# First input projection as three rounded products with split operands, and modulation products with the weights stationary

## The chip, the cores and the metric

The kernel runs on one core of a Trainium2 chip. The metric is the device time of one launch in microseconds (us). A core has TensorE (PE, matrix products; its weight loads are listed apart as PEld), VectorE (DVE), ScalarE (ACT), GpSimd (POOL) and SyncE (SP, here only a DMA queue). Each runs its own instruction list in order and waits on semaphores for the others.

## The reference, cut to what matters

Two transformer blocks follow each other on 256 latent and 256 context tokens, width 1024, all in float32. The change touches the head of the first one:

```
sh_a, sc_a, gt_a, sh_m, sc_m, gt_m = split(silu(cond) @ ada_w + ada_b, 6)   # twice: c, c_ctx; 2 layers
h = rms_norm(x) * (1 + sc_a) + sh_a                                          # 512 rows x 1024
qa, ka, va, qb, kb, vb, ob, g = split(h @ w_in)     # 7 blocks of 512 columns, and 16 gate columns
```

qa, ka, va go to a windowed attention (8 heads of 64) and a context attention; qb, kb, vb, ob and the 16 gates g (4 kinds by 4 heads) to a bidirectional chunked recurrence (mLSTM), whose gates pass tanh, softplus and running sums. Both outputs are merged and projected by ab_w_out, and an MLP follows.

## The kernel before, in words

Weights come through a ring of three buffers ("slabs", 2 MB: 1024 rows by 512 columns). SP issues them in the order of one list, and a slab waits until the one three places earlier is used. The list begins with four slabs of ada_w (modulation part 0), then the eight of ab_w_in (seven of 512 columns, the last of 16), then eight (part 1) and twelve (part 2) of ada_w, then ab_w_out.

*Modulation* (`ada_matmuls`, L665). Both condition vectors are held stationary: `csil` holds silu(c), silu(c_ctx) in two of its 46 columns and zeros elsewhere, so that a slice of it puts slab i's result on rows 2i and 2i+1. One slab is eight products with 8 to 24 stationary columns and 512 moving columns (L680). In the trace each float32 product is two records. The bias enters by one more product (L674). ACT copies the rows out (L698), PE turns them (L709), DVE copies the columns (L719). The generator yields after each product, and `fill(pe, queue, n)` (L688) takes n of them and so puts them between other work: part 0 (32 products) in the prologue, part 1 two by two between the 32 attention units, part 2 as 24 products ahead of the gate decays and then two by two in the recurrence (`ml_pe`, L1177), 36 times.

*First projection* (`ab_in_pe`, L756; `rows_pe`, L557). Per slab and token tile (four of 128) eight float32 products accumulate in one PSUM bank, hT stationary, weights moving: 7 x 4 x 8 = 224 products. The 16 gate columns come last: four groups with 4 stationary columns, 8 products each (L763), in banks 4 to 7. ACT copies each bank out (L776 to L782), then the gates' tanh (L1035). DVE squares and reduces qa and ka beside that (L794, L796). After it eight normalised tiles are turned (L833) and scaled (L812), then attention begins: scores (L857), turned probabilities (L865), values (L877), filler.

*Split products elsewhere.* Later matrices already run as three products in the rounded type fp32r: ACT rounds a slab (high, L336), DVE subtracts (low, L343), and PE adds x_high·w_high, x_low·w_high and x_high·w_low (L380, L1366, L1381, L2249).

*After attention.* Softplus (ACT), decays (DVE, ACT), 48 small products (L1114, L1120), turns of qb and kb (L1165), then per head h of four: L1185, filler, L1191, DVE's masks (L1249), and eight steps L1202, L1203, L1205, filler. Then the merge (L1325) and ab_w_out (L557).

Of the kernel before, what the change touches and what calls it, by code (L numbers as in the profile page):

```python
# [106 lines left out]
def bidir_dual_stack(nc, a, out, scratch_mod, scratch_rpb, noted):  # L107
    const_at, n_const = constant_columns()

    with ExitStack() as ctx:  # L110
# [55 lines left out]
        sc = sb("sc", [P, 6, 512])  # L166
# [13 lines left out]
        with ExitStack() as same_place:  # L180

            hT = same_place.enter_context(nc.sbuf_tensor("hT", [P, KT, 2 * T], F32))
            ring = same_place.enter_context(nc.sbuf_tensor("ring", [P, RING, SLAB], F32))
            arena = same_place.enter_context(nc.sbuf_tensor("arena", [P, ARENA], F32))
        hT_parts = sb("hT_parts", [P, KT, 2 * T], F32R)
        ring_parts = sb("ring_parts", [P, RING, SLAB], F32R)
        arena_parts = sb("arena_parts", [P, ARENA], F32R)
        psum = ctx.enter_context(nc.psum_tensor("psum", [P, 8, 512], F32))
# [55 lines left out]
        plan_rows("ab_in", a["ab_w_in"][0], KT, 3600)  # L244
# [274 lines left out]
        def first_mod_dve(dve):  # L519
# [6 lines left out]
            for k in range(KT):  # L526
                dve.wait_ge(*when(("read", ("L0a", k // 2))))
                dve.wait_ge(*when(("read", ("C0a", k // 2))))
                for v in range(2):
                    h = hT[:, k, 256 * v:256 * v + 256]  # L530
                    shift = mcol(0, v, 0)
                    nc.vector.tensor_scalar(h, h, plus1[v][:, k:k + 1], shift[:, k:k + 1], ALU.mult, ALU.add)\
                        .then_inc(*up(dve, ("first", k) if v else None))

# [37 lines left out]
        csil = area(23136, KT, 46)  # L572
# [3 lines left out]
        def setup_sp(sp):  # L576
# [6 lines left out]
                .then_inc(landing("vec_b"), 16)  # L583

# [5 lines left out]
        def setup_pool(pool):  # L590
            nc.gpsimd.memset(csil, 0.0).then_inc(*up(pool, "csil zero"))
            pool.wait_ge(*latest(pool))
# [4 lines left out]
            for part, (layer, n0, ns, base) in enumerate(ADA_PARTS):  # L597
                for v in range(2):
                    nc.gpsimd.dma_start(adab[base + v:base + 2 * ns:2, :],
                                        a["ada_b"][layer, 512 * n0:512 * (n0 + ns)].rearrange("(i f) -> i f", f=512))\  # L600
                        .then_inc(landing(f"ada_b {part}"), 16)
# [14 lines left out]
            nc.gpsimd.dma_start(stat[0:4, 200:204], a["ab_gate_b"][0].rearrange("(a b) -> b a", b=4), allow_slow_non_contiguous=True)\  # L616
                .then_inc(landing("gate_b"), 16)
# [21 lines left out]
        def setup_pe(pe):  # L639
            pe.wait_ge(*when(("dma", "const")))  # L640
            for i, (rows, ev) in enumerate(((ROWS_A, "vec_a"), (ROWS_B, "vec_b"))):
# [3 lines left out]
                nc.tensor.transpose(psum[:, i, 0:n], sc[0:n, i, 0:P], ident[0:n, 0:n]).then_inc(*up(pe, ("vec", "turned", i)))  # L645

        def setup_dve(dve):
            for i, (col, rows) in enumerate(((colA, ROWS_A), (colB, ROWS_B))):
# [3 lines left out]
                dve.wait_ge(*latest(dve))  # L652

        def setup_act(act):
            act.wait_ge(*when(("read", ("vec", 1))))
            act.wait_ge(*when("csil zero"))
            for i, name in enumerate(("c", "c_ctx")):
                nc.scalar.activation(csil[:, :, 22 + i], colB[:, ROWS_B[name]:ROWS_B[name] + 8], ACT.Silu).then_inc(*up(act, "silu c"))
                act.wait_ge(*latest(act))


        ADA_PARTS = ((0, 0, 4, 64), (0, 4, 8, 32), (1, 0, 12, 0))
        ADA_BANK = (2, 6, 0)

        def ada_matmuls(pe, part):  # L665
            layer, n0, ns, base = ADA_PARTS[part]
            rows = psum[0:2 * ns, ADA_BANK[part], :]
            stage(pe, "ada")
            pe.wait_ge(*bank(ADA_BANK[part], ("ada", part)))
            pe.wait_ge(*when("silu c"))  # L670
            pe.wait_ge(*when(("dma", f"ada_b {part}")))
            pe.wait_ge(*when(("dma", "const")))
            at = slice(base, base + 2 * ns)
            nc.tensor.matmul(rows, ident[at, at], adab[at, :], start=True, stop=False)  # L674
            for i in range(ns):
                name = (f"ada{layer}", n0 + i, 0)
                for k in range(KT):
# [4 lines left out]
                    if k == KT - 1:  # L682
# [11 lines left out]
        def ada_rows_act(act, part):  # L694
            stage(act, "ada")
            layer, n0, ns, base = ADA_PARTS[part]
            act.wait_ge(*when(("ada", "full", part)))
            nc.scalar.copy(adab[base:base + 2 * ns, :], psum[0:2 * ns, ADA_BANK[part], :])\  # L698
                .then_inc(*up(act, ("read", ("ada", part))))
            also(("ada", "rows", part), ("read", ("ada", part)))  # L700

        def ada_turn_pe(pe, part, b):
            stage(pe, "ada")
            layer, n0, ns, base = ADA_PARTS[part]
            at = slice(base, base + 2 * ns)
            pe.wait_ge(*when(("ada", "rows", part)))
            pe.wait_ge(*bank(b, ("mod", part)))
            for j in range(4):
                ins = nc.tensor.transpose(psum[:, b, 2 * ns * j:2 * ns * j + 2 * ns], adab[at, P * j:P * j + P], ident[at, at])  # L709
            ins.then_inc(*up(pe, ("mod", "turned", part)))  # L710

        def ada_turn_dve(dve, part, b):
            stage(dve, "ada")
            layer, n0, ns, base = ADA_PARTS[part]
            dve.wait_ge(*when(("mod", "turned", part)))
            src = psum[:, b, 0:8 * ns].rearrange("p (j i v) -> p v i j", j=4, v=2)
            for v in range(2):
                at = 48 * v + 4 * n0
                ins = nc.vector.tensor_copy(modcol[:, layer, at:at + 4 * ns].rearrange("p (i j) -> p i j", j=4), src[:, v])  # L719
                ins.then_inc(*up(dve, ("read", ("mod", part)) if v else None))  # L720
            dve.wait_ge(*latest(dve))

        def ada_store_pool(pool, part):
            stage(pool, "ada")
            layer, n0, ns, base = ADA_PARTS[part]
            pool.wait_ge(*when(("ada", "rows", part)))
            for v in range(2):
                nc.gpsimd.dma_start(scratch_mod[layer][v, 512 * n0:512 * (n0 + ns)].rearrange("(i f) -> i f", f=512),
                                    adab[base + v:base + 2 * ns:2, :])\
# [23 lines left out]
        AB = ("qa", "ka", "va", "qb", "kb", "vb", "so")  # L753
        rowg = ("i_f", "f_f", "i_b", "f_b")

        def ab_in_pe(pe):  # L756
            rows_pe(pe, "ab_in", lambda k, t: hT[:, k, P * t:P * t + P], range(4), KT, 3584, [0, 1, 2, 3], each="first")
            stage(pe, "ab")
            s = slab(pe, ("ab_in", 7, 0))
            for g in range(4):  # L760
                pe.wait_ge(*bank(4 + g, ("gates", g)))
                for k in range(KT):
                    ins = nc.tensor.matmul(psum[0:4, 4 + g, :], s[:, k, 4 * g:4 * g + 4], hT[:, k, :],  # L763
                                           start=(k == 0), stop=(k == 7))
                ins.then_inc(*up(pe, ("gates", "full", g)))
            also(("used", slab_at[("ab_in", 7, 0)]), ("gates", "full", 3))

        def ab_in_act(act):
            stage(act, "ab_in")
            for n, name in enumerate(AB):  # L770
                for t in range(4):
                    act.wait_ge(*when(("ab_in", "full", n, t)))
                    src = psum[:, t, :]
                    event = ("read", ("ab_in", n, t))
                    if name == "so":
                        ins = nc.scalar.activation(so[:, t, :], src, ACT.Sigmoid)  # L776
                    elif name == "kb":
                        ins = nc.scalar.activation(kb[:, t, :], src, ACT.Copy, scale=128 ** -0.5)
                    elif name == "vb":
                        ins = nc.scalar.copy(vb[:, t, :, 0:128], src.rearrange("p (h d) -> p h d", h=4))  # L780
                    else:
                        ins = nc.scalar.copy({"qa": qa, "ka": ka, "va": va, "qb": qb}[name][:, t, :], src)  # L782
                    ins.then_inc(*up(act, event))


        def qk_norm_dve(dve):
            stage(dve, "qk")
            for i in range(8):
                y = (qa, ka)[i % 2][:, i // 2, :].rearrange("p (h d) -> p h d", h=8)
                sq = sc[:, i % 2, :].rearrange("p (h d) -> p h d", h=8)  # L790
                dve.wait_ge(*when(("read", ("ab_in", i % 2, i // 2))))
                if i < 2:
                    dve.wait_ge(*when(("C0a", "turned", 3)))
# [3 lines left out]
                dve.wait_ge(*latest(dve))  # L797
            for i in range(8):
# [229 lines left out]
        def gates_act(act):  # L1028
# [3 lines left out]
            act.wait_ge(*when(("dma", "rpb rows")))  # L1032
            for g in range(4):
                act.wait_ge(*when(("gates", "full", g)))
                nc.scalar.activation(capped[g], psum[0:4, 4 + g, :], ACT.Tanh, bias=stat[0:4, 204 + g:205 + g],  # L1035
                                            scale=1 / 15.0).then_inc(*up(act, ("read", ("gates", g))))
# [2114 lines left out]
```

## Time and profile before

| | |
|---|---|
| median of 3 runs | 3432.3 us (3430.59 to 3435.97) |
| profiled execution | 3440.02 us, span 3438.2 us |
| PE busy | 3122.3 us, 91% of the span |
| DVE, ACT, POOL busy | 49%, 28%, 8% |
| mean granted TensorE clock | 0.941 |

The span is the stretch between the first and last instruction. A row of the view by windows reads: stretch, its length, then busy us (and instructions) of PE, PEld, DVE, ACT and POOL, the granted PE clock (1.00 is 2.4 GHz, 0.50 is 1.2 GHz), the busy share of the DMA engines, GB/s. A row of the timeline reads: start, us from first start to last end, engine, line, operation, out<-in, shape, count, and in brackets the idle time ahead. The duration of a matmul record includes its latency, so the cost of one in a stream is the distance from start to start.

### The profile page before, as it was taken

How to read it: one execution, taken by the hardware profiler on the slowest of the kernel's cores; microseconds unless marked ns; L12 is line 12 of the kernel's file. 1: busy time of each engine (PE TensorE's matmuls, PEld its weight loads, DVE VectorE, ACT ScalarE, POOL GpSimd, SP SyncE). 2: the span in 40 equal slices, each digit the busy share in tenths (PEclk: the TensorE clock that was granted, in tenths of full speed). 3: DMA queues.
4: the chain of work that ended last, by engine and by line, in shares of the span. 5: the costliest groups of instructions: out<-in, count | busy, mean ns of one | idle time of the engine just before them, and what ended most of it. 6: DMA issues, size and time to landing. Idle time of an engine off the chain costs nothing. (4 is left out here: it accounts for less than half of the span.)

```text
span 3438.2 us, 54550 instructions
## 1 busy us (share of the span) xinstructions
PE 3122.3 (91%) x24312; PEld 2324.8 (68%) x24312; DVE 1697.6 (49%) x2689; ACT 963.3 (28%) x1489; POOL 282.4 (8%) x362
## 2 busy tenths in 40 slices
PE   7999988799996977989978989999899999998899
PEld 2443333398994536888866979874579898455697
DVE  1104356465556108777755555455445453465453
ACT  1012310133331115443312333322223332142332
POOL 1202011000000012232310000000000000200000
PEclk9998989899998988999979999999999999999999
DMA  8311344245453210000024545542245554323253
GB/s 252 102 55 62 135 147 172 73 147 196 172 196 95 92 25 2 3 3 3 4 81 141 193 150 172 187 165 89 98 144 168 165 183 169 128 74 123 74 192 128
DMA packets 249827, 409.23 MB, mean 119 GB/s; under 512 B 10055, under 2 KB 102616, under 8 KB 249464
## 3 DMA queue, kind: packets, MB, share of 16 engines
q1 hardware_dynamic: 244824, 390.39, 33.3%
q0 software_dynamic: 4768, 15.35, 1.8%
q8 instruction: 191, 3.13, 0.4%
q14 instruction: 44, 0.36, 0.0%
HBM read 400.67 MB, written 2.95 MB: 117 GB/s over the span
## 5 line engine op out<-in xcount | busy, mean ns | idle before, releaser
L343 DVE TENSOR_TENSOR ring_parts<-ring,arena_parts 128x2048 fp32r<-128x2048 f32 x250 | 553.0, 2254 | 276.9 <-ACT arena_parts L336 274.6
L336 ACT CAST arena_parts<-ring 128x2048 fp32r<-128x2048 f32 x250 | 457.3, 1879 | 601.3 <-PE psum L2249 229.5
L2249 PE MATMUL psum<-arena_parts 128*128 128x256 f32 x2816 | 514.8, 286 | 6.4 <-DVE arena_parts L452 6.2
L2249 PEld LDWEIGHTS psum<-arena_parts 128*128 128x128 f32 x2816 | 444.0, 194 | 9.2 <-DVE arena_parts L452 9.2
L557 PE MATMUL psum<-ring,hT 128*128 128x512 f32 (+1 forms) x960 | 414.2, 593 | 9.1 <-DVE hT L1308 2.6
L2249 PE MATMUL psum<-arena_parts,ring_parts 128*128 128x256 f32 x1408 | 400.8, 285 | 0.0
L557 PEld LDWEIGHTS psum<-ring,hT 128*128 128x128 f32 x960 | 184.0, 192 | 234.5 <-issue 223.1
L380 PE MATMUL psum<-arena_parts 128*128 128x512 f32 x928 | 291.9, 396 | 8.3 <-DVE arena_parts L2285 8.1
L2249 PEld LDWEIGHTS psum<-arena_parts,ring_parts 128*128 128x128 f32 x1408 | 272.9, 194 | 0.0
L1381 PE MATMUL psum<-arena_parts 128*128 128x512 f32 x768 | 240.5, 395 | 7.8 <-DVE arena_parts L1428 7.8
L380 PEld LDWEIGHTS psum<-arena_parts 128*128 128x128 f32 x928 | 176.8, 191 | 46.6 <-DVE arena_parts L2285 9.0
L680 PE MATMUL psum<-ring,arena 128*24 128x512 f32 (+2 forms) x384 | 188.4, 625 | 3.1 <-DMA ring<-in_ada_w 3.1
L1366 PE MATMUL psum<-arena_parts 128*128 128x256 f32 x1024 | 187.9, 286 | 3.6 <-DVE arena_parts L446 3.6
L380 PE MATMUL psum<-ring_parts,arena_parts 128*128 128x512 f32 x464 | 182.6, 394 | 0.0
L1381 PEld LDWEIGHTS psum<-arena_parts 128*128 128x128 f32 x768 | 145.7, 191 | 38.5 <-DVE arena_parts L1428 8.4
L1366 PEld LDWEIGHTS psum<-arena_parts 128*128 128x128 f32 x1024 | 162.3, 195 | 5.1 <-DVE arena_parts L446 4.7
L1381 PE MATMUL psum<-ring_parts,arena_parts 128*128 128x512 f32 x384 | 151.3, 394 | 0.0
L1366 PE MATMUL psum<-arena_parts,ring_parts 128*128 128x256 f32 x512 | 146.0, 285 | 0.0
L2280 DVE TENSOR_TENSOR sc<-sc,psum 128x512 f32<-128x512 f32 x44 | 30.3, 688 | 228.5 <-PE psum L2249 228.5
L2731 PE MATMUL psum<-ring,hT 128*128 128x512 f32 x256 | 126.9, 626 | 1.3 <-DMA ring<-in_xmem_wkv 1.3
L416 POOL TENSOR_SCALAR stat<-stat 128x2 f32<-128x2 f32 x17 | 3.6, 210 | 1479.0 <-issue 1167.2
L471 PE MATMUL psum<-const,sc 128*128 128x128 f32 x240 | 52.9, 395 | 68.9 <-DVE sc L428 68.9
(407 smaller groups left out, 5095.4 us busy)
## 6 DMA issues: line engine op xcount, KB each, us to landing
ring<-in_mlp_w SPq DMA_DIRECT2D x48, 2048.0 KB, 7.8
ring<-in_ada_w SPq DMA_DIRECT2D x24, 2048.0 KB, 8.0
ring<-in_ffn_pre_w_gu SPq DMA_DIRECT2D x44, 1024.0 KB, 6.9
ring<-in_ffn_post_w_gu SPq DMA_DIRECT2D x44, 1024.0 KB, 7.1
ring<-in_ffn_pre_w_down SPq DMA_DIRECT2D x8, 2048.0 KB, 7.9
ring<-in_xmem_wkv SPq DMA_DIRECT2D x8, 2048.0 KB, 8.1
ring<-in_ffn_post_w_down SPq DMA_DIRECT2D x8, 2048.0 KB, 7.8
ring<-in_ab_w_in SPq DMA_DIRECT2D x7, 2048.0 KB, 8.3
```

The lines of the kernel that those rows point to most:

```text
L336: nc.scalar.copy(high_view(name)[:, k, :], raw_view(name)[:, k, :]).then_inc(*up(act, ("high", name, h)))
L343: nc.vector.tensor_tensor(low_view(name)[:, k, :], raw_view(name)[:, k, :], high_view(name).bitcast(F32)[:, k, :], ALU.subtract)\
L380: ins = nc.tensor.matmul(psum[:, b, :], lhs[q][:, k0 + k, P * t:P * t + P], s[:, k, :], start=(k0 + k == 0 and i == 0), stop=(k0 + k == kt ...
L416: nc.gpsimd.tensor_scalar(s[:, 2:4], s[:, 0:2], 1.0 / D, EPS, ALU.mult, ALU.add).then_inc(*up(pool))
L471: ins = nc.tensor.transpose(psum[:, b + 4, at:at + 128], sc[:, 2 * t + k // 4, 128 * (k % 4):128 * (k % 4) + 128], ident)
L557: ins = nc.tensor.matmul(psum[:, where[t], 0:w], lhs(k0 + k, tile), s[:, k, 0:w], start=(k0 + k == 0), stop=(k0 + k == kt - 1))
L680: ins = nc.tensor.matmul(rows, csil[:, k, 22 - 2 * i:22 - 2 * i + 2 * ns], s[:, k, :], start=False, stop=(i == ns - 1 and k == KT - 1))
L1366: ins = nc.tensor.matmul(psum[:, b, 256 * j:256 * j + 256], s[:, k, at:at + P], src[q][:, k, :], start=(k == 0 and i == 0), stop=(k == 7 a ...
L1381: ins = nc.tensor.matmul(psum[:, b, :], hid_groups[g % 2][q][:, k, P * t:P * t + P], s[:, k, :], start=(g == 0 and k == 0 and i == 0), sto ...
L2249: ins = nc.tensor.matmul(psum[:, b, 256 * j:256 * j + 256], s[:, k, at:at + P], x_parts[q][:, k, :], start=(k == 0 and i == 0), stop=(k == ...
L2280: nc.vector.tensor_tensor(t, t, psum[:, 2 * (n % 2) + 1, :], ALU.mult)\
L2731: ins = nc.tensor.matmul(psum[:, 6 + i, :], hT[:, k, 256 + P * i:256 + P * i + P], s[:, k, :], start=(k == 0), stop=(k == KT - 1))
```

## The change: what it does

- *First projection*: order of the blocks 0, 1, 2, 3, 4, 5, 7 (gates), 6. Each weight slab is split in two halves (k 0 to 3, 4 to 7): ACT rounds a half into `ab_high` (two places, one for each half), DVE writes the rest into `ring_parts`. The rows are split as well: ACT rounds hT[k] into `ab_high_x`, DVE subtracts in place. Three fp32r products take the place of each float32 one, over halves, so that all four token tiles of a block end with its second half. Blocks alternate between banks 0 to 3 and 4 to 7.
- *Gates*: DVE zeroes a 128-column area and puts the four groups at columns 0, 32, 64, 96; 24 products with 128 stationary columns give all of them in bank 4; tanh reads partitions 32g. Block 6 reuses the place that held the gates' high part.
- *Modulation*: the slab is stationary, 32 products per slab (8 k by 4 columns groups of 128) with 128 stationary and 2 moving columns. DVE adds the bias from a turned copy. One `fill` unit is now eight products, and a slab has four units: the fills are 17 in the prologue, 1 between attention units, 12 ahead of the decays, 1 in the recurrence. The turns to rows (parts 1 and 2, only for the gate vectors' use) and their ACT copies, POOL stores and waits move: part 1 ahead of the decays, part 2 after the merge.
- *DVE*: squares of qa, ka go between the splits of blocks 3 and 4.

```diff
-                for k in range(KT):
-                    s = slab(pe, name)
-                    ins = nc.tensor.matmul(rows, csil[:, k, 22 - 2 * i:22 - 2 * i + 2 * ns], s[:, k, :],
-                                           start=False, stop=(i == ns - 1 and k == KT - 1))
+                for j in range(4):
+                    s = slab(pe, name)
+                    at = 8 * i + 2 * j
+                    for k in range(KT):
+                        ins = nc.tensor.matmul(psum[:, b, at:at + 2], s[:, k, P * j:P * j + P], sil[:, k, :],
+                                               start=(k == 0), stop=(k == KT - 1))
...
+        def ab_high_act(act, n, h):
+            act.wait_ge(*when(("ab padded") if n == 7 else ("slab", slab_at[("ab_in", n, 0)])))
...
+            if n == 6 and h == 1:
+                act.wait_ge(*when(("ab used", 5, 1)))
+            elif n:
+                act.wait_ge(*when(("ab used", AB_ORDER[AB_ORDER.index(n) - 1], h)))
+            nc.scalar.copy(ab_high_at(n, h), ab_raw(n, h)).then_inc(*up(act, ("ab high", n, h)))
...
         def ab_in_pe(pe):
+            for i, n in enumerate(AB_ORDER):
+                for h in range(1 if n == 7 else 2):
+                    pe.wait_ge(*when(("ab low", n, h)))
...
+                    for k in range(4 * h, 4 * h + 4):
+                        for t in range(4):
+                            for j, (w, y) in enumerate(((high, ab_high_x), (high, hT_parts), (low, ab_high_x))):
+                                ins = nc.tensor.matmul(psum[:, b, :], y[:, k, tile], w[:, k - 4 * h, :],
...
-            fill(pe, ada[0], 16)
             first_turn_pe(pe, "L0a")
             fill(pe, ada[0], 8)
             first_turn_pe(pe, "C0a")
-            fill(pe, ada[0], 8)
-            fill(pe, ada[0], 1)
-            ada_turn_pe(pe, 0, 3)
+            fill(pe, ada[0], 9)
             ab_in_pe(pe)
             qk_norm_pe(pe)
-            att_pe(pe, "na", na, [("read", ("qkT", i)) for i in range(8)], ada[1], 2)
-            att_pe(pe, "cx", cxa, (), ada[1], 2)
+            att_pe(pe, "na", na, [("read", ("qkT", i)) for i in range(8)], ada[1], 1)
+            att_pe(pe, "cx", cxa, (), ada[1], 1)
             fill(pe, ada[1], 1)
-            fill(pe, ada[2], 24)
+            fill(pe, ada[2], 12)
+            ada_turn_pe(pe, 1, 7)
             decay_pe(pe)
```

## Rows read from the trace of the kernel before

**Rows 1.** Windows: the stretches that the change reaches.
```profile
54.20:276.00 221.80, 221.74 (x513) 91.14 (x513) 21.47 (x34) 19.79 (x32) 29.23 (x21) 0.99 0.31 88
286.90:310.90 24.00, 22.10 (x45) 8.57 (x46) 10.55 (x23) 7.07 (x16) 15.29 (x34) 0.50 0.00 0
311.20:371.30 60.10, 60.10 (x246) 24.90 (x243) 24.70 (x57) 19.11 (x49) 0.00 (x0) 1.00 0.31 105
371.40:428.50 57.10, 55.82 (x193) 19.82 (x192) 17.53 (x64) 16.95 (x64) 0.00 (x0) 0.97 0.43 148
428.60:450.30 21.70, 21.70 (x51) 4.97 (x50) 15.42 (x45) 4.30 (x6) 1.13 (x2) 1.00 0.82 286
467.70:593.00 125.30, 114.13 (x384) 44.95 (x384) 77.08 (x272) 5.04 (x8) 14.94 (x25) 0.92 0.39 134
```

**Rows 2.** Waits of PE from 50 to 620 us: total, times, longest.
```profile
PE psum L1202 <- DVE sc L1249: 11.2, 4, 2.8
PE psum L1114 <- ACT arena L1103: 4.4, 1, 4.4
```

**Rows 3.** Timeline: first modulation product, end of part 0, first projection product.
```profile
17.75 15.45 PE L680 MATMUL psum<-ring,arena 128*8 128x512 f32 x32 [3.06 <-DMA ring<-in_ada_w]
...
50.96 0.57 ACT L698 COPY adab<-psum 8x512 f32<-8x512 f32 x1 [6.17 <-PE psum L680]
...
54.26 66.31 PE L557 MATMUL psum<-ring,hT 128*128 128x512 f32 x150 [2.26 <-DVE hT L532]
```

**Rows 4.** Groups by line, PE, 54 to 276 us.
```profile
L557 PE MATMUL psum<-ring,hT 128*128 128x512 f32 x448 | 194.2, 596 | 2.3 <-DVE hT L532 2.3
L763 PE MATMUL psum<-hT,ring 128*4 128x512 f32 x64 | 27.6, 592 | 0.0
```

**Rows 5.** Timeline of a later split projection, 512 moving columns.
```profile
2271.40 0.62 PE L380 MATMUL psum<-arena_parts 128*128 128x512 f32 x2
...
2272.08 0.62 PE L380 MATMUL psum<-arena_parts 128*128 128x512 f32 x2
```

**Rows 6.** Groups of the page: the two steps of a split, half a slab.
```profile
L343 DVE TENSOR_TENSOR ring_parts<-ring,arena_parts 128x2048 fp32r<-128x2048 f32 x250 | 553.0, 2254 | 276.9 <-ACT arena_parts L336 274.6
L336 ACT CAST arena_parts<-ring 128x2048 fp32r<-128x2048 f32 x250 | 457.3, 1879 | 601.3 <-PE psum L2249 229.5
```

**Rows 7.** Timeline: products with 4 moving columns, and what follows.
```profile
458.18 3.55 PE L1120 MATMUL psum<-arena,const 4*128 4x4 f32 x16
461.66 5.15 PE L1165 MATMUL psum<-const,arena 128*128 128x128 f32 x32
```

**Rows 8.** Timeline: products with 64 moving columns, and what follows.
```profile
2316.62 3.68 PE L2429 MATMUL psum<-arena 128*128 128x64 f32 x32
2320.13 3.65 PE L2731 MATMUL psum<-ring,hT 128*128 128x512 f32 x8
```

**Rows 9.** Windows around the small products and the turns.
```profile
455.00:461.20 6.20, 6.20 (x47) 6.20 (x46) 0.00 (x0) 0.00 (x0) 0.00 (x0) 0.50 0.42 158
461.70:464.60 2.90, 2.90 (x15) 2.90 (x15) 0.32 (x1) 1.26 (x3) 2.06 (x4) 0.50 0.00 0
464.80:466.00 1.20, 1.20 (x14) 1.20 (x13) 0.00 (x0) 1.20 (x3) 1.01 (x3) 1.00 0.00 0
```

**Rows 10.** Timeline: one early attention unit, from its scores to its filler.
```profile
294.97 2.07 PE L857 MATMUL psum<-arena 64*128 64x512 f32 x2
296.98 1.11 PE L865 MATMUL psum<-const,sc 128*128 128x128 f32 x4
298.02 1.97 PE L877 MATMUL psum<-sc,arena 128*64 128x128 f32 x8
299.92 1.88 PE L674 MATMUL psum<-adab,const 16*16 16x512 f32 x2
```

**Rows 11.** Timeline: one early step of the recurrence.
```profile
475.38 0.80 PE L1202 MATMUL psum<-arena,sc 128*128 128x129 f32 x2 [2.79 <-DVE sc L1249]
...
476.97 3.60 PE L680 MATMUL psum<-ring,arena 128*24 128x512 f32 x4
480.50 0.80 PE L1202 MATMUL psum<-arena,sc 128*128 128x129 f32 x2
```

More of the change, by code:

```diff
@@ L533, in first_mod_dve, with low_x, first_high_act @@
                         .then_inc(*up(dve, ("first", k) if v else None))
+            def low_x(k):
+                dve.wait_ge(*when(("first high", k)))
+                nc.vector.tensor_tensor(hT_parts[:, k, :], hT[:, k, :], ab_high_x.bitcast(F32)[:, k, :], ALU.subtract)\
+                    .then_inc(*up(dve, ("first", "low", k)))
+            modulated(0)
+            for k in range(1, KT):
+                modulated(k)
+                low_x(k - 1)
+            low_x(KT - 1)
+        def first_high_act(act):
+            stage(act, "norm")
+            for k in range(KT):
+                act.wait_ge(*when(("first", k)))
+                nc.scalar.copy(ab_high_x[:, k, :], hT[:, k, :]).then_inc(*up(act, ("first high", k)))
         def rows_pe(pe, name, lhs, tiles, kt, n_total, banks, needs=(), only=None, each=None):
@@ L692, in fill, with ada_cols_dve @@
             stage(pe, held)
[L694 to L700, printed above, removed]
+        def ada_cols_dve(dve, part):
+            stage(dve, "ada")
+            layer, n0, ns = ADA_PARTS[part]
+            dve.wait_ge(*when(("ada", "full", part)))
+            src = psum[:, ADA_BANK[part], 0:8 * ns].rearrange("p (c v) -> p v c", v=2)
+            for v in range(2):
+                at = 48 * v + 4 * n0
+                nc.vector.tensor_tensor(modcol[:, layer, at:at + 4 * ns], src[:, v],
+                                        colC[:, 48 * layer + 4 * n0:48 * layer + 4 * n0 + 4 * ns], ALU.add)\
+                    .then_inc(*up(dve, ("read", ("ada", part)) if v else None))
+            also(("mod", part), ("read", ("ada", part)))
+            dve.wait_ge(*latest(dve))
@@ L702, in ada_turn_pe @@
         def ada_turn_pe(pe, part, b):
             stage(pe, "ada")
-            layer, n0, ns, base = ADA_PARTS[part]
-            at = slice(base, base + 2 * ns)
-            pe.wait_ge(*when(("ada", "rows", part)))
+            layer, n0, ns = ADA_PARTS[part]
+            pe.wait_ge(*when(("mod", part)))
             pe.wait_ge(*bank(b, ("mod", part)))
-            for j in range(4):
-                ins = nc.tensor.transpose(psum[:, b, 2 * ns * j:2 * ns * j + 2 * ns], adab[at, P * j:P * j + P], ident[at, at])
+            for v in range(ADA_ROWS[part][1]):
+                at = 48 * v + 4 * n0
+                ins = nc.tensor.transpose(psum[0:4 * ns, b, P * v:P * v + P], modcol[:, layer, at:at + 4 * ns], ident)
@@ L710, in ada_turn_pe, with ada_rows_act @@
             ins.then_inc(*up(pe, ("mod", "turned", part)))
[L712 to L721, printed above, removed]
+        def ada_rows_act(act, part, b):
+            stage(act, "ada")
+            layer, n0, ns = ADA_PARTS[part]
+            at, nv = ADA_ROWS[part]
+            act.wait_ge(*when(("mod", "turned", part)))
+            nc.scalar.copy(adab[0:4 * ns, at:at + P * nv], psum[0:4 * ns, b, 0:P * nv])\
+                .then_inc(*up(act, ("read", ("mod", part))))
@@ L723, in ada_store_pool @@
         def ada_store_pool(pool, part):
             stage(pool, "ada")
[L725 to L729, printed above, removed]
+            layer, n0, ns = ADA_PARTS[part]
+            at, nv = ADA_ROWS[part]
+            pool.wait_ge(*when(("read", ("mod", part))))
@@ new lines, in ab_low_dve, with ab_pad_dve @@
+        def ab_low_dve(dve, n, h):
+            stage(dve, "ab_split")
+            dve.wait_ge(*when(("ab high", n, h)))
+            nc.vector.tensor_tensor(ab_low(n, h), ab_raw(n, h), ab_high_at(n, h).bitcast(F32), ALU.subtract)\
+                .then_inc(*up(dve, ("ab low", n, h)))
+        def ab_pad_dve(dve):
+            stage(dve, "ab_split")
+            dve.wait_ge(*when(("slab", slab_at[("ab_in", 7, 0)])))
+            v = raw_view(("ab_in", 7, 0))
+            nc.vector.memset(v[:, :, P:2 * P], 0.0).then_inc(*up(dve))
+            dve.wait_ge(*latest(dve))
+            for g in range(4):
+                nc.vector.tensor_copy(v[:, :, P + 32 * g:P + 32 * g + 4], v[:, :, 4 * g:4 * g + 4])\
+                    .then_inc(*up(dve, "ab padded"))
@@ L766, in ab_in_pe @@
-            also(("used", slab_at[("ab_in", 7, 0)]), ("gates", "full", 3))
-        def ab_in_act(act):
[L769 to L783, printed above, removed]
@@ new lines, in ab_out_act @@
+        def ab_out_act(act, i):
+            n = AB_ORDER[i]
+            stage(act, "ab_in")
+            name = AB[n]
+            for t in range(4):
+                act.wait_ge(*when(("ab_in", "full", n, 3 if name == "so" else t)))
+                src = psum[:, t + (4 * (i % 2) if n != 6 else 0), :]
+                event = ("read", ("ab_in", n, t))
+                if name == "so":
+                    ins = nc.scalar.activation(so[:, t, :], src, ACT.Sigmoid)
+                elif name == "kb":
+                    ins = nc.scalar.activation(kb[:, t, :], src, ACT.Copy, scale=128 ** -0.5)
+                elif name == "vb":
+                    ins = nc.scalar.copy(vb[:, t, :, 0:128], src.rearrange("p (h d) -> p h d", h=4))
+                else:
+                    ins = nc.scalar.copy({"qa": qa, "ka": ka, "va": va, "qb": qb}[name][:, t, :], src)
+                ins.then_inc(*up(act, event))
@@ new lines, in ab_in_act, with ab_in_dve @@
+        def ab_in_act(act):
+            for i, n in enumerate(AB_ORDER):
+                if i < 7:
+                    ab_high_act(act, AB_ORDER[i + 1], 0)
+                if n == 7:
+                    gates_act(act)
+                else:
+                    ab_out_act(act, i)
+                if i < 7 and AB_ORDER[i + 1] != 7:
+                    ab_high_act(act, AB_ORDER[i + 1], 1)
+        def ab_in_dve(dve):
+            for n in AB_ORDER[1:]:
+                if n == 7:
+                    ab_pad_dve(dve)
+                ab_low_dve(dve, n, 0)
+                if n != 7:
+                    ab_low_dve(dve, n, 1)
+                if n in (3, 4):
+                    qk_squares_dve(dve, range(4 * n - 12, 4 * n - 8))
@@ L797, in qk_norm_dve @@
                 dve.wait_ge(*latest(dve))
+        def qk_norm_dve(dve):
+            stage(dve, "qk")
             for i in range(8):
@@ L1032, in gates_act @@
             act.wait_ge(*when(("dma", "rpb rows")))
+            act.wait_ge(*when(("gates", "full")))
             for g in range(4):
-                act.wait_ge(*when(("gates", "full", g)))
-                nc.scalar.activation(capped[g], psum[0:4, 4 + g, :], ACT.Tanh, bias=stat[0:4, 204 + g:205 + g],
-                                            scale=1 / 15.0).then_inc(*up(act, ("read", ("gates", g))))
+                rows = slice(32 * g, 32 * g + 4)
+                nc.scalar.activation(capped[g], psum[rows, 4, :], ACT.Tanh, bias=stat[rows, 204:205],
+                                            scale=1 / 15.0).then_inc(*up(act, ("read", "gates") if g == 3 else None))
                 act.wait_ge(*latest(act))
@@ L1135, in rope_pool @@
                 pool.wait_ge(*when(("ab_in", "full", 6, t)))
-            pool.wait_ge(*when(("gates", "full", 3)))
             for y in (qb, kb):
@@ L2922, in _ @@
             first_out_act(act)
-            ada_rows_act(act, 0)
+            for h in range(2):
+                ab_high_act(act, 0, h)
+            first_high_act(act)
             ab_in_act(act)
-            gates_act(act)
-            att_act(act, "na", na, 0.125, [("gates", "full", 3)])
+            att_act(act, "na", na, 0.125, [("ab_in", "full", 6, 3)])
             att_act(act, "cx", cxa, 0.125)
-            ada_rows_act(act, 1)
             softplus_act(act)
+            ada_rows_act(act, 1, 7)
             decay_act(act)
@@ L2989, in _ @@
             first_out_dve(dve)
-            ada_turn_dve(dve, 0, 3)
+            for h in range(2):
+                ab_low_dve(dve, 0, h)
+            ada_cols_dve(dve, 0)
             first_mod_dve(dve)
             gates_dve(dve)
+            ab_in_dve(dve)
             qk_norm_dve(dve)
```

129 lines of the change are left out of this document (83 added, 46 removed).

## The prediction

> **What bounds the kernel now.** I read the shares, then PE's waits, then windows over the stretches that the diff touches, then the timeline inside them, and last the granted clock. PE issues nearly without pause: 221.74 of 221.80 us in the first projection, all of the attention from 311 us on, 21.70 of 21.70 us in the filler ahead of the decays [rows 1]. Its waits between 50 and 620 us are few: 2.8 us per head of the recurrence and 4.4 us for the decays [rows 2]. So up to the merge the time is the sum of what PE issues, and everything is priced there. The reader is to see three more things. The projection's 448 and the gates' 64 records cost 0.43 us each (194.2/448, 27.6/64) [rows 4]. The clock is not the same everywhere: it is 0.50 (1.2 GHz) through the first 24 us of attention although PE is busy for 22 of them, and 1.00 after [rows 1]. And products with 4 moving columns ran at 0.50 for 6.20 us without one gap, while the 128-column turns behind them had the clock at 1.00 within about 3 us [rows 9].
>
> **First projection: less work.** 224 float32 products become 672 rounded ones. Three of these take 2272.08 - 2271.40 = 0.68 us, 0.227 each [rows 5]: 152.4 us, against 194.2. The gates go from 27.6 to 24 x 0.227 = 5.4 us. The splits: half a slab costs ACT 1.88 and DVE 2.25 us [rows 6], while PE works 10.9 us on a half (48 products). ACT's high part of the next block's second half waits for the end of the present block and for four copies of its banks; that is some 7 us with DVE's part, under the 10.9 us of the next first half. It is hidden, DVE's squares too. One place has no cover: block 6's first half needs the place of the gates' high part, which is free only when the gates are done. Then ACT 1.88 + DVE 2.25 + handovers = 4.4 us of idle PE (zero is excluded, nothing of PE's lies there; twice that if ACT is late). The clock may fall in such a gap; I add 1.7, an estimate: the 3 us or so that the turns took to raise it [rows 9], half of it lost. New length 163.9 us against 221.8: -58. Bounds: -62 (no clock loss) and -29 (each slab's splits exposed once, 7 x 4.1 us). The tail (turns L833, start of attention) keeps its shape.
>
> **Modulation: the same PE time at the high clock, twice that at the low one.** One slab was 16 records at 0.43 = 6.9 us. It is now 32 products of 128 stationary and 2 moving columns, 64 records. No row has 128 x 128 stationary and 2 moving. The nearest two: 64 moving columns at the high clock, (2320.13 - 2316.62)/32 = 0.110 us per record [rows 8]; 4 moving columns at the low clock, (461.66 - 458.18)/16 = 0.2175 [rows 7]. They differ by two, as the clocks do, and hardly by the moving columns, so the weight load sets them. A slab costs 7.0 us at 2.4 GHz and 13.9 us at 1.2 GHz. There is nothing to win at either, only the bias products go.
>
> The stationary block of the L1120 row has 4 rows, the new one 128. By the Trainium skill (TensorE: Matmul & The Clock Gate, section "LDWEIGHTS (loading the stationary operand)") a load takes time by its columns and not by its rows; by that the 0.2175 holds for the new products, and the L2429 row with its 128 rows, at half of it, agrees.
>
> So the question is the clock. What speaks: with 4 moving columns PE had no gap for 6.20 us and stayed at 0.50 [rows 9]. With 64-row scores, turns and 16-column filler it stayed at 0.50 for 24 us [rows 1]. I take it that the new products leave the clock low, as the small ones did; between the attention's own work (under 5 us per unit at the low clock [rows 10]) they then stand like pauses, and that stage needed 24 us to get to the high clock even with its old filler. I take 0.50 for the prologue, both attentions, the filler and the recurrence.
>
> - Prologue: first product at 17.75, end of part 0 at 50.9 [rows 3]. Now 4 slabs at 13.9 less some 4 us that the turns beside them hold the clock up, and 3.4 for the second turns: end at 73; the chain to the first projection product (bias add, plus one, modulate, round, subtract) is about 4.5 us where it was 3.3: 77.5 against 54.3. +23. Bounds -2 and +30.
> - First attention (84.4 us, of which 60.1 at 1.00 [rows 1]). A unit's own work at the low clock is 299.92 - 294.97 = 4.95 us [rows 10], plus 16 x 0.2175 = 3.48: 16 units are 135, +51. Where turns and values come together the clock may come back for a while: I take +43. Bounds -1 and +51.
> - Context attention (57.1). Less 32 x 1.72 of filler halves: (57.1 - 27.5)/16 = 1.85 own work, up to 3.4 at the low clock, plus 3.48: 110, +53. Gaps don't double: +43. Bounds -1 and +53.
> - Filler ahead of the decays: 21.7 + 4.4 = 26.1 us [rows 1, 2] was set by DVE's and ACT's decays. Twelve units are 41.8 us and now outlast them. ACT's copy of part 1's rows waits for PE's turn behind the filler, and the exponentials stand behind that copy, so the 4.4 comes again: 46.2, +20. With the high clock (20.9) nothing changes.
> - Recurrence: 125.3/4 = 31.3 us per head [rows 1]. A step at the low clock is 476.97 - 475.38 = 1.59 [rows 11] + 3.48 = 5.07; eight of them 40.6, one filler 3.5, L1185 1.7, four records of L1191 3.4, the wait 2.8 [rows 2]: 52. +20.8 per head, +83. Bounds -8 (DVE, busy 77.08 of 125.30 us [rows 1], sets a floor soon under the present pace) and +90.
> - After the merge DVE's columns of part 2, PE's turn and no ACT wait ahead of ab_w_out: +1. SP's list keeps its order and every slab its place; at 14 us a slab DMA has time.
>
> **Sum.** +23 - 58 + 43 + 43 + 20 + 83 + 1 = +155 us. On the profiled execution 3440.0 + 155 = 3595; it lies 7.7 above the median of the runs, so against the median 3432.3 + 155 = 3587. Faster in the projection, much slower in everything that the filler shares.
>
> **Rivals.**
> - *Loads hold the clock (faster).* The new filler keeps the granted clock as the old one did. For it: PE issues without a gap, and the 4-column rows have 4 stationary rows too, so they don't tell loads of 128 rows apart. Against: the 24 us at 0.50 with a busy PE. Prologue -1, projection -58, attentions -2, decays 0, recurrence -1, tail +1: -61, 3371. Decided at the first 12-unit filler: above 0.9 there, and it holds everywhere. Chance 0.28. The Trainium skill (same page, section "What's actually happening") says that the clock follows how busy PE has been recently and that activity releases the throttle; read plainly that is this rival, and rows 9 are what stands against it.
> - *Low clock only in the long runs.* The products of the attentions hold the clock between fillers; it falls in the prologue, the long filler and the recurrence: +23 - 58 - 2 + 20 + 83 + 1 = +67, 3499. For it: from 311 to 371 us the same products stood at 1.00. Chance 0.04. If the recurrence holds as well it is -16, 3416. Chance 0.02.
> - *The rounded products don't do what they say,* bound by the splits: the -29 above with the clock held, 3400. For it: two engines and a semaphore chain per half slab. Against: later stages do the same at 0.227. Chance 0.02.
>
> **How the numbers follow.** Forecast 0.64 at 3587, its own range 3535 to 3630 (the terms of attention and recurrence each between full cold and a third won back). Loads hold the clock 0.28, the others as above. Faster (by over 0.2%, which is about what a measurement tells from no change) holds in 0.28 + 0.02 + 0.02 = 0.32, slower in 0.64 + 0.04 = 0.68; I keep 0.01 of these for no change. To leave out no more than 2 in 10 the range has to hold the fast case: 3362 to 3630.
>
> **What would show it.** The windows of the new kernel: granted clock 0.5 in the 12-unit filler, which is then 42 us long; about 0.22 us per L1120-like record; the first projection's products 0.227 apart and one gap of some 4 us behind the gates; the first of them at 77 us; the recurrence's steps 5 us apart. Wrong would be: 0.11 us per modulation record and clock 1.0 in that filler (then 3371), or a projection that waits for low parts in each slab.

## The result, and the profile after

The changed kernel takes 3579.8 us (median of 4 runs, 3578.75 to 3581.53) against 3431.45 us (median of 4, 3427.79 to 3435.97). The ratio is 1.0432, 95% interval 1.0414 to 1.0450: slower by 148 us, in a forecast of +155. Its profiled execution took 3581.53 us, span 3579.7, mean granted TensorE clock 0.878 where it was 0.941.

First the shares and the slices of the span. Per engine: busy us, share of the span, instructions; then 40 equal slices, the granted clock in tenths.

```profile
PE 3264.0 (91%) x25634; PEld 2699.4 (75%) x25634; DVE 1733.9 (48%) x2721; ACT 995.9 (28%) x1511; POOL 281.3 (8%) x357
...
PEclk6985555579999899899997999999989999999899
```

PE is busy for 91% as before, but for 142 us more, and five slices in a row show half the clock. The windows say what stood there (stretch, length, busy us of PE, PEld, DVE, ACT, POOL, granted clock, DMA share, GB/s): first projection, first attention, context attention, filler, recurrence. They stand beside [rows 1].

```profile
78.70:249.80 171.10, 166.64 (x696) 134.26 (x697) 51.60 (x60) 45.16 (x49) 30.07 (x21) 0.97 0.40 114
262.10:387.60 125.50, 124.12 (x480) 93.42 (x478) 35.26 (x80) 25.03 (x64) 13.88 (x31) 0.54 0.15 51
387.60:485.30 97.70, 97.18 (x369) 76.49 (x369) 17.52 (x64) 17.37 (x63) 0.00 (x0) 0.50 0.25 87
485.40:529.80 44.40, 44.40 (x210) 44.40 (x210) 15.71 (x47) 3.85 (x5) 0.00 (x0) 0.50 0.41 142
557.00:742.40 185.40, 177.72 (x788) 169.72 (x788) 75.41 (x264) 3.78 (x6) 15.31 (x24) 0.50 0.26 91
```

The projection is 51 us shorter and runs at the high clock. Everything that shares PE with modulation products is longer, at 0.50 to 0.54, with PE busy nearly throughout. In the filler PE was busy for 44.40 of 44.40 us, loading for all of it, and had 0.50. The timeline (start, us from first start to last end) shows the pieces: both halves of the prologue, the first projection product, one unit of the context attention, the filler and what follows, one step of the recurrence.

```profile
17.95 26.54 PE L701 MATMUL psum<-arena,ring 128*128 128x2 f32 x128 [2.22 <-DMA ring<-in_ada_w]
44.35 3.65 PE L502 MATMUL psum<-const,arena 128*128 128x128 f32 x16
47.80 27.30 PE L701 MATMUL psum<-arena,ring 128*128 128x2 f32 x128
78.79 0.77 PE L850 MATMUL psum<-sc_parts,arena_parts 128*128 128x512 f32 x1 [3.69 <-issue]
...
442.58 1.22 PE L972 MATMUL psum<-arena 64*128 64x256 f32 x2
443.72 0.69 PE L980 MATMUL psum<-const,sc 128*128 128x128 f32 x2
444.34 1.12 PE L992 MATMUL psum<-sc,arena 128*64 128x128 f32 x4
445.39 3.58 PE L701 MATMUL psum<-arena,ring 128*128 128x2 f32 x16
...
485.36 44.53 PE L701 MATMUL psum<-arena,ring 128*128 128x2 f32 x208
529.75 0.59 PE L737 MATMUL psum<-const,modcol 128*32 128x128 f32 x2
535.39 3.58 PE L1232 MATMUL psum<-const,arena 4*128 4x4 f32 x32 [5.05 <-ACT arena L1221]
...
550.50 1.84 PE L701 MATMUL psum<-arena,ring 128*128 128x2 f32 x16
...
561.77 0.78 PE L1319 MATMUL psum<-arena,sc 128*128 128x129 f32 x2
562.34 0.64 PE L1320 MATMUL psum<-arena,sc 128*128 128x129 f32 x2
562.77 0.64 PE L1322 MATMUL psum<-sc,arena 128*128 128x129 f32 x2
563.20 3.42 PE L701 MATMUL psum<-arena,ring 128*128 128x2 f32 x16
566.48 0.78 PE L1319 MATMUL psum<-arena,sc 128*128 128x129 f32 x2
```

The filler's 208 records take (529.75 - 485.36)/208 = 0.213 us each. One unit happened to fall into a stretch at the high clock (550.50): 16 records in 1.77 us, 0.111 each. So the new product has the two prices of [rows 7] and [rows 8], and which one it has goes with the clock. PE's waits from 50 to 780 us (total, times, longest) hold few things that are new:

```profile
PE psum L1319 <- DVE sc L1366: 10.4, 4, 2.8
PE psum L1442 <- DVE arena L1418: 10.4, 4, 9.4
PE psum L1232 <- ACT arena L1221: 5.0, 1, 5.0
PE psum L850 <- DVE ring_parts L812: 4.4, 1, 4.4
PE psum L850 <- issue: 3.7, 1, 3.7
```

### The profile page after: what moved, and what is told of

It is laid out like the page before. It is cut to its first block and busy times, and to the rows that moved or that the text cites. A ratio compares the mean times of both kernels' runs of the same rounds, so it can differ in the third digit from the quotient of the medians.

```text
span 3579.7 us, 57242 instructions
## 1 busy us (share of the span) xinstructions
PE 3264.0 (91%) x25634; PEld 2699.4 (75%) x25634; DVE 1733.9 (48%) x2721; ACT 995.9 (28%) x1511; POOL 281.3 (8%) x357
## 5 line engine op out<-in xcount | busy, mean ns | idle before, releaser
L701 PEld LDWEIGHTS psum<-arena,ring 128*128 128x128 f32 x1536 | 327.3, 326 | 12.7 <-issue 12.7
L701 PE MATMUL psum<-arena,ring 128*128 128x2 f32 x1536 | 325.7, 345 | 2.2 <-DMA ring<-in_ada_w 2.2
L577 PE MATMUL psum<-ring,hT 128*128 128x512 f32 (+1 forms) x512 | 220.3, 592 | 4.3 <-DVE hT L2300 1.6
L577 PEld LDWEIGHTS psum<-ring,hT 128*128 128x128 f32 x512 | 98.6, 194 | 121.9 <-issue 114.6
```

Source lines behind the costliest of these rows:

```text
L577: ins = nc.tensor.matmul(psum[:, where[t], 0:w], lhs(k0 + k, tile), s[:, k, 0:w], start=(k0 + k == 0), stop=(k0 + k == kt - 1))
L701: ins = nc.tensor.matmul(psum[:, b, at:at + 2], s[:, k, P * j:P * j + P], sil[:, k, :], start=(k == 0), stop=(k == KT - 1))
```

## The experiments

Two theories. *Clock:* modulation products with 2 moving columns leave the clock low, and their low clock also doubles the work that stands between them; the projection gains by itself. *Rivals:* a 128 x 128 float32 load is slow at any clock; or the splits cost something that the sum doesn't hold. Each run was timed in rounds beside the kernel before on the same chip.

### Each part alone

`e1_projection_alone` puts the old modulation back:

```diff
-                        ins = nc.tensor.matmul(psum[:, b, at:at + 2], s[:, k, P * j:P * j + P], sil[:, k, :],
+                    ins = nc.tensor.matmul(rows, csil[:, k, 22 - 2 * i:22 - 2 * i + 2 * ns], s[:, k, :],
...
-            ada_cols_dve(dve, 0)
+            ada_turn_dve(dve, 0, 3)
```

> New projection (split operands, padded gates, squares between the splits) with the modulation as it was before: csil stationary, 512 moving columns, the fills and turns of before. Theory (the slowdown is the clock that the modulation products with 2 moving columns leave low): the projection is shorter by 52 us (50.6 measured, 2.4 of cold start in it back, 1 for rounding and subtracting ahead of it), everything behind it as before: 3431 - 52 = 3379, 3370 to 3388. The first attention runs at the clock of before. Rival (the splits on ACT and DVE or the rounded products cost part of the slowdown, here or behind the projection): 3400 or more.

Measured: 3379.68 us, ratio 0.9844 (0.9829 to 0.9859). `e2_modulation_alone` is the other half, the kernel before with the new modulation:

```diff
-                    ins = nc.tensor.matmul(rows, csil[:, k, 22 - 2 * i:22 - 2 * i + 2 * ns], s[:, k, :],
+                        ins = nc.tensor.matmul(psum[:, b, at:at + 2], s[:, k, P * j:P * j + P], sil[:, k, :],
```

> New modulation (slab stationary, 2 moving columns) with the float32 projection of before. Theory: all of the loss and none of the gain, so 3431 + 148 + 52 = 3631, 3620 to 3645, with the granted clock 0.5 in both attentions, in the filler ahead of the decays and in the recurrence. Rival (projection and modulation disturb each other, the parts don't add up): more than 15 us away from 3631.

Measured: 3634.04 us, ratio 1.0572 (1.0545 to 1.0599). The parts add up: -54 and +201 give +147, the change measured +148. The splits cost nothing that shows. The slices of the clock, first with the projection alone, then with the modulation alone:

```profile
PEclk9989998999998979999979999999899999998999
```

```profile
PEclk8996555559999989799897999999989999999899
```

The five slices at half the clock go with the modulation.

### The same products with more moved columns

`e3_128_moving` leaves the change as it is and only widens the moving operand:

```diff
-                        ins = nc.tensor.matmul(psum[:, b, at:at + 2], s[:, k, P * j:P * j + P], sil[:, k, :],
+                        ins = nc.tensor.matmul(psum[:, b, at:at + MOVED], s[:, k, P * j:P * j + P], wide[:, 2 * k:2 * k + MOVED],
```

> The changed kernel, except that each modulation product moves 128 columns in place of 2 (silu(c), silu(c_ctx) and 126 columns of later pairs and zeros, whose results are written beside and overwritten or not read). Same weight loads, same number of instructions. Theory (few moved columns leave the clock low): the clock is held, a record costs 0.11 us, which the load sets anyway, so more work for PE makes the kernel faster: 3377, 3365 to 3390; granted clock above 0.9 in the 13-unit filler. Rival (a load of 128 x 128 float32 costs 0.21 us here at any clock, or stationary weights from the ring are slow for another reason): stays at 3580 or above.

Measured: 3377.84 us, ratio 0.9837 (0.9822 to 0.9852); once more, on another chip (`e3_again`), 3377.27, 0.9827 (0.9813 to 0.9840).

> The kernel with 128 moving columns once more, on the same chip as the other three, so that differences of a few us can be read: 3378.

Sixty-four times as many columns moved, none of the added ones of use, make the changed kernel 202 us faster. The filler, in the timeline and as a window:

```profile
375.14 23.49 PE L706 MATMUL psum<-arena,ring 128*128 128x128 f32 x208
```

```profile
375.20:398.60 23.40, 23.40 (x211) 23.35 (x210) 15.72 (x47) 3.86 (x5) 0.00 (x0) 1.00 0.77 268
```

The number of records is that of the change, 0.112 us apart at clock 1.00. The rival of slow loads falls: the loads are the same. With 32 columns:

> As the run with 128 moving columns, but 32. Theory: it is the amount of moved columns that counts, and a quarter of the engine's time moving them is still too little where nothing else stands beside them: clock 0.5 in the 13-unit filler, somewhat better in the attentions; 3540, 3480 to 3580. Rival (2 columns were a special case, any real number of columns holds the clock): about 3377, as with 128.

Measured: 3545.99 us, ratio 1.0358 (1.0301 to 1.0414). The filler stays where it was, (490.08 - 445.69)/208 = 0.213 us per record. What is won lies in the first attention, which took 348.74 - 259.66 = 89.1 us where the change took 126.7.

```profile
445.69 44.58 PE L706 MATMUL psum<-arena,ring 128*128 128x32 f32 x208
```

### 64 columns: a miss, and what it taught

> As the run with 128 moving columns (gates in the place that the change gave them), but 64. With 32 the clock stood at 0.5 in the 13-unit filler and the time was 3546. Theory (the amount of moved columns decides, and it is a step, not a slope: a stretch runs at one of two clocks): 64 is enough, 3377 as with 128, the record set by its load at 0.11 us. Rival (the time slopes with the columns): half way, about 3480.

Measured: 3522.64 us (3513.89 to 3538.11), ratio 1.0264 (1.0238 to 1.0290). Neither theory holds. In its trace one kind of record has two prices:

```profile
45.11 3.62 PE L502 MATMUL psum<-const,arena 128*128 128x128 f32 x16
48.52 14.48 PE L706 MATMUL psum<-arena,ring 128*128 128x64 f32 x128
...
429.47 3.68 PE L706 MATMUL psum<-arena,ring 128*128 128x64 f32 x16
434.13 44.64 PE L706 MATMUL psum<-arena,ring 128*128 128x64 f32 x208
```

Both groups run without a gap. The first, behind turns (L502) at whose end the clock had risen, goes at 0.113 us per record (14.48/128); the second came in at the low clock and stays there at 0.215 (44.64/208). What stood ahead seems to decide. But the number of columns counts at the same place too. Behind the same turns, first with 2 columns (`e2_modulation_alone`), then with 32 (`e4_32_moving`), the products began at the high clock as well and had lost it by 52 us, with PE busy throughout, where those with 64 kept it for all of 14.5 us:

```profile
48.30:51.00 2.70, 2.70 (x26) 2.70 (x26) 0.00 (x0) 0.59 (x1) 0.00 (x0) 1.00 1.05 405
52.00:55.00 3.00, 3.00 (x15) 3.00 (x16) 0.00 (x0) 0.00 (x0) 0.00 (x0) 0.50 0.04 12
```

```profile
48.80:51.00 2.20, 2.20 (x23) 2.20 (x21) 0.00 (x0) 0.81 (x2) 0.00 (x0) 1.00 1.05 410
52.00:55.00 3.00, 3.00 (x16) 3.00 (x16) 0.00 (x0) 1.24 (x1) 0.00 (x0) 0.50 0.33 116
```

`e9_64_after_128` tests what a raised clock is worth to 64 columns, by a few wide units at the places where it had been lost:

```diff
+        WARM = {1: (16, 17, 18), 2: (0, 1, 2, 13, 14, 22, 23, 31, 32, 40, 41)}
...
+                    MOVED = P if 4 * i + j in WARM.get(part, ()) else 64
```

> The expectation for 64 columns failed (3523 in place of 3377). Its trace has the same products at both clocks: 0.113 us apart behind turns that had raised the clock (second half of the prologue, most of the first attention), 0.215 apart for 44.6 us in the filler, which it entered with the clock low. New theory: 64 moved columns are enough to keep a raised clock but not to raise it. Here 11 to 14 of the 96 units move 128 columns (the first three of the context attention, the first three of part 2, the second and third step of the recurrence in each head), all others 64. Theory: these raise the clock and the 64 behind them keep it: context attention 58 us, filler 26, recurrence near 130; the prologue's first half stays cold, which is 13 us more than with 128 throughout: 3396, 3385 to 3415. Rival (64 columns lose the clock after a while whatever came before; what was held in the first attention was held by the attention's own products): above 3480.

Measured: 3392.83 us (3388.56 to 3405.34), ratio 0.9890 (0.9870 to 0.9910). Fourteen units of 96 differ from the run with 64 columns, and 130 us are gone. The context attention's first unit with 128 columns is slow, the second fast, and those with 64 behind it stay fast; so do the filler (its wide ones are its second to fourth, the clock was up when it began; a timeline row names only the first shape of its group) and the steps of the recurrence:

```profile
355.10 3.36 PE L707 MATMUL psum<-arena,ring 128*128 128x128 f32 x16
...
359.97 2.05 PE L707 MATMUL psum<-arena,ring 128*128 128x128 f32 x16
...
367.08 2.00 PE L707 MATMUL psum<-arena,ring 128*128 128x64 f32 x16
...
406.61 23.44 PE L707 MATMUL psum<-arena,ring 128*128 128x64 f32 x208
...
457.93 3.07 PE L707 MATMUL psum<-arena,ring 128*128 128x128 f32 x16
461.51 1.95 PE L707 MATMUL psum<-arena,ring 128*128 128x128 f32 x16
463.96 1.90 PE L707 MATMUL psum<-arena,ring 128*128 128x64 f32 x16
```

Behind the wide units the rival, a clock that 64 columns lose after a while, does not hold: the context attention kept it from its fourth unit on, and so did the nine units of 64 alone (16 us) at the filler's end. But the theory is not general. The same trace has a stretch where products with 64 columns, the first of the prologue, began at the high clock and lost it while PE was busy:

```profile
18.20:19.40 1.20, 1.20 (x13) 1.20 (x13) 1.20 (x3) 0.00 (x0) 0.00 (x0) 1.00 1.04 384
20.60:23.00 2.40, 2.40 (x14) 2.40 (x13) 0.00 (x0) 0.00 (x0) 0.00 (x0) 0.50 1.05 387
```

Ahead of them PE had waited 1.2 us for the first slab; whether that is why, no run tests. And the first attention, all 64 columns in both runs, took 103.2 us here (clock 0.50 until about 309 us) and 83.1 us in the trace of `e7_64_moving` (low until about 274). Why the clock came back so much later is open; it made the profiled execution, 3405.34 us, the slowest of the four.

### Two waits taken away

`e5_gates_last` and `e6_128_gates_last` put the gates behind block 6:

```diff
-        AB_ORDER = (0, 1, 2, 3, 4, 5, 7, 6)
+        AB_ORDER = (0, 1, 2, 3, 4, 5, 6, 7)
...
-                pe.wait_ge(*bank(4 + i % 4, ("qkT", i)))
+                pe.wait_ge(*bank(4 + (i + 1) % 4, ("qkT", i)))
```

> New projection with the old modulation (as the first run of this study), but the gates' block last again, behind block 6, and the turns of qa and ka begin in bank 5, so that none waits for the tanh. Theory: the 4.4 us in which PE waits behind the gates are there because block 6's first half has to wait for the place of the gates' high part; with the gates last its splits lie beside block 5, the gap goes, and with it the stretch at the low clock behind it (about 2.5 us): 7 us off, 3373 against 3380. The split of the gates, with DVE's five small steps ahead of it, lies beside block 6 then. Rival (the gap moves to the gates, or comes back ahead of attention): 3380, no change.

> Both: 128 moving columns in the modulation products, and the gates' block last. If the two are independent: 3378 - 7 = 3371, the fastest so far; rival: 3378.

Measured: 3372.38 us, ratio 0.9821 (0.9808 to 0.9835), and 3367.88, 0.9807 (0.9794 to 0.9821), where the kernel with 128 columns alone had 3377.27 on that chip. The intervals overlap, as do those of `e5_gates_last` and `e1_projection_alone` (0.9829 to 0.9859, another chip); the traces tell more. ab_w_out starts at 548.96 us where it started at 556.82 with the projection alone, and at 547.94 where it started at 557.34 with 128 columns (`e3_again`). The wait of 4.4 us is gone from both, and the clock stays up where it had fallen. The same place, first with the gates last, then ten microseconds of it with the gates seventh (`e1_projection_alone`):

```profile
198.00:222.00 24.00, 22.66 (x104) 18.26 (x102) 5.24 (x7) 6.83 (x10) 2.16 (x5) 1.00 0.33 110
```

```profile
198.00:208.00 10.00, 6.22 (x17) 4.93 (x18) 6.14 (x5) 7.20 (x7) 0.00 (x0) 0.66 0.68 242
```

From first product to first turn the projection took 226.17 - 53.57 = 172.6 us with 128 columns (`e3_128_moving`) and 218.05 - 53.88 = 164.2 with the gates last besides. The two traces with 128 columns and the gates seventh hold one wait more for the low part of a slab, of 1.0 and 2.0 us at about 102 us, where the prologue had ended 25 us earlier than in the change.

`e8_turn_later` also moves part 1's turn and ACT's copy of it behind the decays:

```diff
-            ada_turn_pe(pe, 1, 7)
             decay_pe(pe)
+            ada_turn_pe(pe, 1, 2)
...
-            ada_rows_act(act, 1, 7)
             decay_act(act)
+            ada_rows_act(act, 1, 2)
```

> 128 moving columns, gates last, and part 1's turn to rows behind the decays' small products in place of ahead of them, ACT's copy of the rows behind the exponentials (bank 2). Theory: in the changed kernel PE waits 5.0 us between the 13-unit filler and the decays, because the exponentials stand behind ACT's copy, which waits for the turn behind the filler. Without that the decays are bound by DVE's and ACT's own chain, 26 us from the start of the filler as in the kernel before; the filler is 23.5, so 2.6 are left: 2.5 us off, 3365 against 3368. Rival (the exponentials wait for DVE and not for the copy): the 5.0 stays, and no change.

> 128 moving columns and the gates last once more, on the same chip as the run above: 3368.

Measured: 3363.73 us (3362.66 to 3366.21), ratio 0.9810 (0.9794 to 0.9826), beside 3368.20 (3364.07 to 3369.50), 0.9820 (0.9803 to 0.9837). These intervals overlap, so the time alone shows no gain. But the wait went down by what was expected, from 5.0 to

```profile
PE psum L1237 <- ACT arena L1226: 2.4, 1, 2.4
```

and from the start of the filler to ab_w_out it took 541.23 - 366.10 = 175.1 us beside 542.25 - 363.23 = 179.0.

This is the fastest version: 1.9% below the kernel before, 216 us below the change as it was made.

## Why the prediction was right, step by step

It was right in mechanism and in size: the clock stays low in nearly all that the filler shares, the projection gains, the sum is far on the slow side. That the sum came within 7 us owes something to luck: the recurrence, forecast 15.7 too dear, stands against the projection, the filler and the prologue, together 12.8 too cheap. By its terms, each as the difference of starts in the two timelines:

| step | predicted | measured |
|---|---|---|
| start of the first projection | +23 | 78.79 - 54.26 = +24.5 |
| projection | -58 | 171.1 - 221.7 = -50.6 |
| first attention | +43 | 126.7 - 84.5 = +42.2 |
| context attention | +43 | 97.7 - 57.2 = +40.5 |
| filler to decays | +20 | 50.0 - 26.1 = +23.9 |
| recurrence (from L1302, L1185 before) | +83 | 192.9 - 125.6 = +67.3 |
| decays, turns, up to ab_w_out | +1 | +0.4 |

The measured terms give +148.2 at the start of ab_w_out (760.79 - 612.56). The span is only 141.5 longer; the other 6.7 lie behind it, where the change touches nothing. In the traces of this study the part behind that start took between 2817.4 and 2827.8 us, 2825.6 before and 2818.9 after, so the 6.7 are within what it varies by. That they are the 7.7 us by which the profiled run of before stood above its median is likely and not shown; taking the base down to the median in the forecast came out right.

- *Price of a record.* Forecast 0.110 and 0.2175 by clock, measured 0.111 and 0.213, 0.219 in the attention (3.51/16), 0.205 in the recurrence (3.28/16). The load's rows don't matter: the change has 128 where the row at the low clock had 4, and the price is the same. Nor do 2, 32 or 64 moved columns at the low clock (0.213 to 0.215), or 2, 64 or 128 at the high one (0.111 to 0.113), which leaves the load as what sets it.
- *Rival "Loads hold the clock" (0.28)*: refuted. In the filler PE was loading for 44.40 of 44.40 us at 0.50. The Trainium skill (TensorE: Matmul & The Clock Gate, "What's actually happening") has the clock follow how busy PE has been. By the busy share of the profile the trace does not agree: 100% busy stood at 0.50 with 2 columns and at 1.00 with 128.
- *Projection (-58, measured -50.6).* Its mechanism held: one gap of 4.4, all other splits hidden. The sizes of three terms were off. The first 4.8 us run at the low clock, with products 0.427 apart, since the prologue hands over a low clock: 2.4 that I had not counted. Behind the gap (225.04) it stays low until about 230.3, which costs 2.6 and not 1.7. At the high clock the products are (220.28 - 83.94)/587 = 0.2323 apart (from the 13th to the 600th, the last ahead of the gap) and not 0.227, read from only three of them: 696 x 0.0053 = 3.7. That leaves 0.2 open. In the changed kernel the gates' gap is the only one in the projection (4.4 of the 4.5 us in which PE was idle), and the run with the gates last shows its cause.
- *Recurrence (+83, measured +67.3)*: the largest miss, 15.7. I added 16 x 0.2175 to the step's own work in the row of the very first step, 1.59. The step's own work is 1.43 now, since less time passes between its last product and the filler, and a unit of filler is 3.28 and not 3.48: 4.71 us, not 5.07, and 32 x 0.36 = 11.5. What the first head issues ahead of its steps ran at the high clock (the unit at 550.50): 7.5 us and not 11.4, another 3.9.
- *Filler to decays (+20, measured +23.9).* I counted 12 units; the last one of part 1 stands ahead of them, 13 x 3.4 = 44.4 us. And the wait is 5.0, not 4.4, behind 0.6 us of turns. Its cause, the exponentials behind ACT's copy of the turned rows, is borne out by the run with the turn moved, where 2.4 are left.
- *Prologue (+23, measured +24.5).* No 4 us of it were won by the turns: both halves ran at 0.50 from about 20 us on, 26.5 and 27.3 us.
- *Attentions:* within 1 and 3 us. The little that I let come back did: three units of the first attention (at 281.87, 295.68 and 343.46 us) had their filler in 1.95 us in place of 3.58.
- *Tail:* small terms that cancel; the gap ahead of the merge's turns shrank from 10.67 to 9.37, the wait ahead of part 2's turn costs 3.4.
- *Slips in the working*, without weight for the sum: the filler halves of the context attention are 16 x 1.72 = 27.5 (not 32), and the projection without a loss of clock is -58 - 1.7 = -60, not -62.

## What to carry to other kernels

In this kernel filler had two jobs: its own result, and keeping TensorE's clock up for the work between it. Before swapping a wide product for a narrow one with the same load, look in the trace at the granted clock of a stretch of narrow products; if it is the low one, price the neighbours at it too. Where the load sets the pace, moving more columns than needed cost next to nothing at the high clock (0.112 us per record with 128 columns, 0.111 with 2) and can be worth it: here 202 us. And read a pitch from a long run of products, not from three.

## What the runs showed of the hardware that I had not expected

A stream of one and the same kind can run at either clock for tens of us: 64 moved columns per load gave 0.113 us per record for 14.5 us behind turns, and 0.215 for 44.6 us where the clock was down. What stood ahead is part of it, as the run with fourteen wide units shows, but not all: one such stream lost the high clock with PE busy, and the clock of the first attention came back at 274 us in one trace and at 309 us in another.

The times of kernels with few moved columns can spread more than those of the others: 3513.89 to 3538.11 us over 5 runs with 64 columns, 3543.59 to 3586.57 over 4 with 32, 3619.06 to 3634.63 over 4 with the new modulation alone, though only 3578.75 to 3581.53 for the change itself.

The long filler stood at the low clock in both traces with 2 columns and in the one with 32, and at the high clock in all five with 128. That the moved columns and not the loads make this difference is shown; how the chip weighs them is not.
